# An expert weight stream cut into transfers of 1 MB, each with its own landing semaphore

## The reference, cut to what matters

```python
def expert_rows(args):
    xblk, e = args
    gt = jnp.minimum(xblk @ w_gate[e] + b_gate[e], SWIGLU_LIMIT)
    up = jnp.clip(xblk @ w_up[e] + b_up[e], -SWIGLU_LIMIT, SWIGLU_LIMIT)
    hdn = (up + 1.0) * gt * jax.nn.sigmoid(gt * SWIGLU_ALPHA)
    return hdn @ w_down[e] + b_down[e]
```

## Time and profile before

| what | value |
|---|---|
| median of 3 runs (lowest, highest) | 1259.48 us (1254.93, 1263.06) |
| profiled execution, its own time | 1256.86 us |
| its span, first to last instruction | 1255.0 us |
| mean granted TensorE clock | 0.971 |
| TensorE busy with matmuls | 1169.7 us, 93% |
| VectorE, ScalarE busy | 487.4 us, 197.0 us |
| read from HBM | 443.57 MB |
| chain of waits: PE, DMA, DVE | 63%, 21%, 13% |

### The profile page before, as it was taken

How to read it: one execution, slowest core, us unless ns; L and a number is a source line. 1 busy time by engine, 2 the same in 40 slices (tenths; PEclk the granted TensorE clock), 3 DMA queues, 4 the chain that set the end, 5 groups by cost and what they waited for, 6 DMA issues and landing times.

```text
span 1255.0 us, 20776 instructions
## 1 busy us (share of the span) xinstructions
PE 1169.7 (93%) x8462; PEld 568.1 (45%) x8462; DVE 487.4 (39%) x1090; ACT 197.0 (16%) x432; POOL 5.4 (0%) x33
## 2 busy tenths in 40 slices
PE   8999988999999989888899999999999899999896
PEld 6888767875334333333333433333433334343333
DVE  2999997105332322232222332221333222233233
ACT  2144513012111101011100111100111100111012
POOL 0000000000000000000000000000000000000000
PEclk9999998999999988998999999899999999999989
DMA  9542338924999999999999999999999999999994
GB/s 393 233 171 78 132 130 295 357 109 155 392 403 426 426 426 427 427 426 427 426 427 427 399 428 426 426 426 410 414 426 426 425 428 371 423 426 428 425 427 182
DMA packets 37074, 452.62 MB, mean 361 GB/s; under 512 B 5112, under 2 KB 5656, under 8 KB 10080
## 3 DMA queue, kind: packets, MB, share of 16 engines
q1 hardware_dynamic: 35344, 449.02, 86.0%
q10 hardware_dynamic: 1616, 1.82, 0.4%
HBM read 443.57 MB, written 7.25 MB: 359 GB/s over the span
## 4 chain that ended last, share of the span: by engine, by line
PE 63%; DMA 21%; DVE 13%; issue 2%; DVEq 1%; ACT 0%; POOL 0%; SPq 0%; POOLq 0%; ACTq 0%
PE ps L1556 26%; DMA ring<-in_w_experts 20%; PE ps L1599 9%; DVE acts L777 5%; PE ps L1523 3%; PE ps L1318 3%; PE ps L1425 3%; PE ps L1292 2%; PE ps L1482 2%; PE ps L1608 2%; PE ps L1538 2%; PE ps L1566 2%; PE ps L1416 1%; DVE acts L1137 1%; DVE acts L872 1%
## 5 line engine op out<-in xcount | busy, mean ns | idle before, releaser
L1556 PE MATMUL ps<-ring,extra 128*64 128x512 f32 x1824 | 415.6, 607 | 10.3 <-DMA ring<-in_w_experts 8.0
L1556 PEld LDWEIGHTS ps<-ring,extra 128*64 128x64 f32 x1824 | 127.0, 139 | 276.6 <-issue 260.8
L1599 PE MATMUL ps<-ring,extra 128*32 128x256 f32 x3072 | 191.9, 397 | 21.5 <-DMA ring<-in_w_experts 21.4
L1137 DVE TENSOR_TENSOR acts<-ps,acts 128x528 f32<-128x528 f32 x128 | 85.2, 704 | 261.3 <-PE ps L1566 157.6
L1599 PEld LDWEIGHTS ps<-ring,extra 128*32 128x32 f32 x3072 | 94.3, 113 | 114.8 <-issue 36.0
L777 DVE SCALAR_TENSOR_TENSOR acts<-ring,small,acts 128x256 f32<-128x256 f32 x224 | 91.2, 474 | 1.1 <-ACT acts L489 1.1
L1318 PE MATMUL ps<-acts,ring 128*128 128x280 f32 (+1 forms) x320 | 75.3, 394 | 0.3 <-ACT ring L562 0.3
L1318 PEld LDWEIGHTS ps<-acts,ring 128*128 128x128 f32 x320 | 60.5, 190 | 14.2 <-issue 1.0
L1142 DVE TENSOR_SCALAR extra<-ps 128x512 f32<-128x512 f32 x32 | 22.1, 692 | 114.9 <-PE ps L1556 114.9
L1318 PE MATMUL ps<-acts,extra 128*128 128x280 f32 x256 | 61.3, 400 | 1.9 <-DVE acts L759 1.9
L1151 DVE TENSOR_SCALAR extra<-ps 128x512 f32<-128x512 f32 x32 | 22.1, 689 | 95.5 <-PE ps L1556 78.9
(11 more groups left out here) (307 smaller groups left out, 892.0 us busy)
## 6 DMA issues: line engine op xcount, KB each, us to landing
ring<-in_w_experts SPq DMA_DIRECT2D x192, 2048.0 KB, 28.1
ring<-in_w_in_t SPq DMA_DIRECT2D x5, 2048.0 KB, 21.0
extra<-in_w_in_t SPq DMA_DIRECT2D x4, 2048.0 KB, 11.1
extra<-in_w_out_t SPq DMA_DIRECT2D x4, 1024.0 KB, 5.9
ring<-in_w_out_t SPq DMA_DIRECT2D x4, 1024.0 KB, 6.4
ring<-in_state_t SPq DMA_DIRECT2D x8, 512.0 KB, 7.7
ring<-dtx_rows SPq DMA_DIRECT2D x8, 512.0 KB, 6.4
out_ssm_s_t<-ring SPq DMA_DIRECT2D x8, 512.0 KB, 7.0
```

Source lines behind the costliest of these rows:

```text
L1137: TT(both, ps[:, BACK_BANK[m]:BACK_BANK[m] + 2, 0:TN], both, ALU.add).then_inc(ev["acc_done"], 1)
L1556: hs.append(MM(dst, src[:, o:o + HALF], weight(w, p, k, 512 * h_, 512), start=(fresh and kk == 0), stop=(kk == KT - 1), skip_group_check=T ...
L1599: hs.append(MM(dst, src[:, o:o + QUAR], weight(w, p, k, 256 * q, 256), start=(fresh and kk == 0), stop=(kk == KT - 1), skip_group_check=True))
```

## The change

- A transfer is one piece of 1 MB (8 KB per partition, every other 8 KB of the HBM block of a pair) and no longer a pair of 2 MB. There are 384 of them for 192.
- The landing semaphores belong to the 16 places of the ring (`piece_slot`), one each, and TensorE waits for the one of the piece that it multiplies with.
- `stream` waits for one piece to be used and requests its place. `gate_piece` replaces `gate_half` and `gate_used`: TensorE counts it up after each gate piece, the fourth time at the first up matmul (with one pass) or after the last gate piece (with two). `piece_used` keeps its eight counts per expert.
- `prefetch` requests the two pieces of a pair one behind the other.
- The loop of the stream writes out four experts for two, so that the place in the ring is a constant. Experts 2 and 3 stand ahead of it.
- Two semaphores on which nothing waits (`e_ready`, `sy_ready`) are gone.

```diff
-        landed = [[sem(f"pair_landed{par}_{i}") for i in range(NP // 2)] for par in range(2)]
+        landed = [sem(f"piece_landed{k}") for k in range(NQ * 4)]
...
+        def piece_slot(i, p):
+            return (i * 3 + p // 4) % NQ * 4 + p % 4
+        def piece_row(i, p):
+            k = piece_slot(i, p)
+            return ring[:, k * PIECE:(k + 1) * PIECE]
...
-        def expert_pair(e, q):
-            return expert_w[bass.ds(e, 1), q].rearrange("o p n -> p (o n)")
+        def expert_piece(e, p):
+            return expert_w[bass.ds(e, 1), p // 2, :, p % 2 * PIECE:(p % 2 + 1) * PIECE].rearrange("o p n -> p (o n)")
...
             def prefetch(q, i=0):
-                sp.dma_start(pair_row(i, q), expert_pair(i, q)).then_inc(landed[i][q], 16)
+                for p in (2 * q, 2 * q + 1):
+                    sp.dma_start(piece_row(i, p), expert_piece(i, p)).then_inc(landed[piece_slot(i, p)], 16)
...
-            def stream(i, e, par, first=0):
-                for q in range(first, NP // 2):
-                    if q < 2:
-                        sp.wait_ge(ev["piece_used"], i * 8 - 16 + 6 + 2 * q)
-                    elif q < 4:
-                        sp.wait_ge(ev[("gate_half", "gate_used")[q - 2]], i)
+            def stream(i, at, e, first=0):
+                for p in range(first, NP):
+                    if p < 4:
+                        sp.wait_ge(ev["piece_used"], i * 8 - 11 + p)
+                    elif p < 8:
+                        sp.wait_ge(ev["gate_piece"], i * 4 - 7 + p)
                     else:
-                        sp.wait_ge(ev["piece_used"], i * 8 - 8 + 2 * (q - 3))
-                    sp.dma_start(pair_row(i, q), expert_pair(e, q)).then_inc(landed[par][q], 16)
-            stream(1, 1, 1, 2)
+                        sp.wait_ge(ev["piece_used"], i * 8 - 15 + p)
+                    sp.dma_start(piece_row(at, p), expert_piece(e, p)).then_inc(landed[piece_slot(at, p)], 16)
+            stream(1, 1, 1, 4)
             sp.wait_ge(ev["order_ready"], 1)
-            with sp.Fori(0, NE // 2 - 1) as ii:
-                for par in range(2):
-                    e = sp.value_load(order[0:1, bass.ds(ii * 2 + 3 + par, 1)], min_val=0, max_val=NE - 1)
-                    stream(ii * 2 + 2 + par, e, par)
+            for i in (2, 3):
+                stream(i, i, sp.value_load(order[0:1, i + 1:i + 2], min_val=0, max_val=NE - 1))
+            with sp.Fori(0, NE // 4 - 1) as t:
+                for h in range(4):
+                    e = sp.value_load(order[0:1, bass.ds(t * 4 + 5 + h, 1)], min_val=0, max_val=NE - 1)
+                    stream(t * 4 + 4 + h, h, e)
...
             def piece_products(p, b, src, bank, fresh, w):
-                pe.wait_ge(w[1][p // 2], w[2])
+                pe.wait_ge(*w[1][p])
...
             def gate_of(n, w, then):
                 for p in range(4):
                     hs = piece_products(p, 0, xT, 0, False, w)
-                    if n == 1 and p == 1:
-                        hs[-1].then_inc(ev["gate_half"], 1)
+                    if n == 1 and p < 3:
+                        hs[-1].then_inc(ev["gate_piece"], 1)
```

More of the change, by code:

```diff
@@ L217, in build @@
                  "dtc_out dt_mm dt_v dt_exp dt_ready ctap_ready conv_done xtap_ready xtail_out xconv_done xs_pre xa_ready z_out "
-                 "acum_mm meta_v meta_exp decb_ready xtok_mm xdt_ready cb_mm d_ready e_ready ce_ready m_ready xdec_ready "
+                 "acum_mm meta_v meta_exp decb_ready xtok_mm xdt_ready cb_mm d_ready ce_ready m_ready xdec_ready "
                  "y_mm st_mm y_ready hT_ready hT_out kept_out mean_mm cent_ready csq_ready var_mm lr_ready norm_ready conf_ready "
-                 "xs_tr dtx_ready dtx_out sh_new sh_y sy_ready yg_ready ysq_ready yvar_mm yr_ready yn_ready "
+                 "xs_tr dtx_ready dtx_out sh_new sh_y yg_ready ysq_ready yvar_mm yr_ready yn_ready "
                  "wo_y_landed wo_conf_landed wo_used wo_mm acc_ready h_tr hsq_ready hstd_ready xn_ready lg_mm nm_ready topexp "
@@ L223, in build @@
                  "rows_zeroed rows_loaded xg_done sg_tr pick_done gp_ready sc_done gate_done g_ready hdn_ready "
-                 "y_back p_ready acc_done s_ready rank_ready sg_ready sort_mm order_ready o_list sig_ready gate_used gate_half up_first piece_used o_tab f_ready f_out fsq_ready fss_mm frstd_ready iota_ready").split()
+                 "y_back p_ready acc_done s_ready rank_ready sg_ready sort_mm order_ready o_list sig_ready gate_piece up_first piece_used o_tab f_ready f_out fsq_ready fss_mm frstd_ready iota_ready").split()
         ev = {n: sem(n) for n in names}
-        landed = [[sem(f"pair_landed{par}_{i}") for i in range(NP // 2)] for par in range(2)]
+        landed = [sem(f"piece_landed{k}") for k in range(NQ * 4)]
         win_landed = [sem(f"win_landed{i}") for i in range(5)]
@@ L404, in _ @@
                         sp.wait_ge(ev["piece_used"], j * 8 + NE * 8)
-                        for q in range(NP // 2):
-                            sp.dma_start(pair_row(0, q), expert_pair(e, q)).then_inc(landed[0][q], 16)
+                        for p in range(NP):
+                            sp.dma_start(piece_row(0, p), expert_piece(e, p)).then_inc(landed[p], 16)
             for q in range(4):
@@ L990, in _ @@
             last = yT[:, :, SEQ:TN]
-            TT(last, ps[:, 7, 0:KT * NB].rearrange("p (m b) -> p m b", m=KT), sdt, ALU.add).then_inc(ev["sy_ready"], 1)
+            TT(last, ps[:, 7, 0:KT * NB].rearrange("p (m b) -> p m b", m=KT), sdt, ALU.add)
             v.drain()
@@ L1140, in gate_in @@
                 for b in range(2):
-                    v.wait_ge(ev[("gate_done", "gate_used")[b]], n + 1)
+                    if b == 0:
+                        v.wait_ge(ev["gate_done"], n + 1)
+                    else:
+                        v.wait_ge(ev["gate_piece"], n * 4 + 4)
                     TS(ge[:, 512 * b:512 * (b + 1)], ps[:, b, :], LIMIT, None, ALU.min).then_inc(ev["g_ready"], 1)
@@ L1539, in bias, with weights_of @@
                        start=True, stop=False, skip_group_check=True)
-            def weights_of(i, par, n16):
-                return [matrix_at(i, m) for m in range(3)], landed[par], n16
+            def weights_of(i):
+                return ([matrix_at(i, m) for m in range(3)],
+                        [(landed[piece_slot(i, p)], 16 * ((i * 3 + p // 4) // NQ + 1)) for p in range(NP)])
             def weight(w, p, k, c, n):
-                return span(w[0][p // 4] + (p % 4) * PIECE + k * D + c, n)
+                at = w[0][p // 4] + (p % 4) * PIECE + k * D + c
+                return ring[:, at:at + n]
             def piece_products(p, b, src, bank, fresh, w):
-                pe.wait_ge(w[1][p // 2], w[2])
+                pe.wait_ge(*w[1][p])
                 hs = []
@@ L1690, in up_of @@
                         if p == 4:
-                            hs[0].then_inc(ev["gate_used"], 1)
+                            hs[0].then_inc(ev["gate_piece"], 1)
                         hs[-1].then_inc(ev["up_first" if p == 7 else "piece_used"], 1)
@@ L1697, in up_of @@
                         hs = piece_products(p, 1, xT, 0, False, w)
-                        if p % 2:
-                            hs[-1].then_inc(ev[("gate_half", "gate_used")[p // 2]], 1)
+                        hs[-1].then_inc(ev["gate_piece"], 1)
                     for p in range(4, 8):
@@ L1731, in gate_s @@
                         then()
-                    if p == 1:
-                        hs[-1].then_inc(ev["gate_half"], 1)
+                    if p < 3:
+                        hs[-1].then_inc(ev["gate_piece"], 1)
                     if p == 3:
@@ L1833, in first_back @@
                 find_order()
[L1835 to L1838, removed]
+            big_expert(0, weights_of(0), first, first_back, second, True)
+            big_expert(1, weights_of(1), second, lambda: big_back(1, first), None)
+            small_expert(2, weights_of(2), lambda: big_back(2, second), None)
+            small_expert(3, weights_of(3), lambda: small_back(3), count_of(5))
             now = count_of(5)
@@ L1841, in _ @@
                 coming = count_of(i + 3)
-                big_expert(i, weights_of(i, 0, i // 2 * 16 + 16), now, lambda: small_back(i), None)
-                small_expert(i + 1, weights_of(i + 1, 1, i // 2 * 16 + 16), lambda: big_back(i + 1, now), coming)
+                big_expert(i, weights_of(i), now, lambda: small_back(i), None)
+                small_expert(i + 1, weights_of(i + 1), lambda: big_back(i + 1, now), coming)
                 now = coming
@@ L1877, in _ @@
                         bias(2, 96)
-                        w = [0, MAT, 2 * MAT], landed[0], j * 16 + 8 * NE + 16
+                        w = [0, MAT, 2 * MAT], [(landed[p], j * 16 + 16 * (3 * NE // NQ + 1)) for p in range(NP)]
                         gate_of(2, w, lambda: None)
```

## The result

The changed kernel takes 1266.55 us (median of 8 runs, 1263.45 to 1272.27) against 1257.6 us for the kernel before (8 runs, 1251.78 to 1263.06). The ratio is 1.008, with a 95% interval of 1.0058 to 1.0103. It is 8.95 us slower; forecast was 5.1 us faster. The difference is small, but the interval leaves no change out: the forecast had the sign wrong.

What follows compares the result with a forecast made beforehand. The weight stream at 427 GB/s, its losses in four stretches and a fixed tail bound the kernel. Gains at restarts and landings less 0.8% packet cost gave -5.1 us: 1254.5 us against the 1259.5 median, range 1246 to 1270.

Steps and rivals of the forecast that it cites:

- The packets' cost: Weight stream: 8 KB packets in place of 16 KB slow it by 0.8%, taken between 0.4% and 1.4%.
- The sum of the prediction: Stream and TensorE shifts followed to the kernel's end: -5.1 us; -0.2 us with packets at 1.4%.
- The later restarts: Three slow stretches behind the wide experts: 2.06, 2.48 and 4.45 us lost, regained except where TensorE bounds it.
- the bounded part: Fourth stretch, near 1070 us: TensorE limits the regain, so the stream's shift is -5.48 us instead of -5.81.
- The first restart: Stretch near 364 us: one megabyte less waits behind the late request, 2.46 us gained.
- The last landing: End of the weight stream: one small piece left to multiply instead of two, 1.0 us gained.
- Edits costed at nothing: 192 further requests at 0.34 us each on SyncE, prefetch requests, longer loop and waits: hidden, no cost.
- the rival for the slower side: Weight stream: 8 KB packets cost 5.1% on every 2 MB, +32 us in all, 1289 us; chance 0.12.
- The 5.1% of the earlier trace: Start of a transfer into an idle queue: 324.5 ns per 8 KB packet, 5.1% over; outer bound of packet cost.

Runs made afterwards that it cites:

- The split kernel: Kernel before, with only the third of an expert's six pairs requested and landed as two 1 MB transfers; 1256.24 us against 1256.65, ratio 1.0.
- the first experiment: Kernel before with weights laid piece by piece in HBM, so its 2 MB transfers move 8 KB packets; 1267.04 us, ratio 1.0079.
- the even and odd split: Kernel before with each pair moved by two 1 MB transfers of 16 KB packets, for even and odd partitions; 1257.41 us, ratio 0.9996.

## Why the prediction was wrong

What follows counts landings: the time at which the n-th megabyte of expert weights had landed, from the landing semaphores in the traces. Both traces have the clock at 1.00 in 296 to 304 us (first trace of before, second of the changed kernel). The plateau's pace is taken between megabytes 48 and 128; "over the plateau's pace" is the time that a stretch took beyond its megabytes at that pace.

```
                                              before   changed   difference
16th megabyte landed (us)                      296.9     298.1      +1.2
16th to 48th, over the plateau's pace (us)      22.49     19.67     -2.8
plateau, us per megabyte                         2.4785    2.5222   +0.0437
   16th to 48th: x 32                                               +1.4
   48th to 384th: x 336                                            +14.7
48th to 384th, over the plateau's pace           6.71      2.11     -4.6
   of it 160th to 192nd                          0.89      0.24
         232nd to 264th                          0.98      0.19
         288th to 328th                          2.27     -0.09
last landing                                  1238.19   1248.06     +9.9
from there to the end of the span               16.8      15.2      -1.6
span                                          1255.0    1263.3      +8.3
```

**The packets' cost** is the step that failed first: the mechanism was the right one, the term was mis-sized, and its size decides the sign. I took 0.8% between 0.4 and 1.4; the stream is 0.0437/2.4785 = 1.8% slower per megabyte here and 1.6% in the first trace of the changed kernel (2.5184). That is some 15 us over the 336 megabytes where 7.0 us stood. The rows had the answer. A quiet window and the real stream differ by 617.7 - 611.8 = 5.9 ns per packet. I read this as a property of the stream and set the quiet 8 KB packet between the two. But the load adds it to each packet of either size: 2 x (310.2 + 5.9) = 632.2 ns, and 631.0 were measured. The packets' own durations in the traces say the same: from a quiet window to the stream the mean of a 16 KB packet goes from 611.0 to 616.3 ns, that of an 8 KB packet from 309.5 (before) to 314.3 (changed). Like had to be compared with like. The sum of the prediction at 1.6% gives about +1.5 us, and the sign is open.

**The later restarts** are the second. I took 2.06, 2.48 and 4.45 us as lost there, from the rates in windows of 20 us, and let all but the bounded part come back. By the landings only 0.89, 0.98 and 2.27 us lay above the pace of the plateau (the plateau's pace already has the packets of the "instruction" queue in it). The second trace of before gives 0.50, 0.72 and 2.04. The split kernel shows the same disagreement, 3.7 us by the window and 0.3 by the landings. The rate and the share are means over 16 engines, and a transfer has landed when its last engine is done. Engines that are ahead may run dry and cost nothing. The packets in the trace bear no engine, but the 16 counts of a transfer's landing do come apart: in the kernel before the first and the last lie 3.5 us apart in the median from 400 to 600 us and up to 7.5 us behind the first later wide expert. A stretch of 2 us without work on some engines fits into that; that it costs nothing is not shown. What was there did come back, 3.8 of 4.14 us. But part came by the slower stream: with 8 KB packets and the requests of before (the first experiment) 0.72, 0.49 and 0.37 us are left, and with 1 MB transfers requested late 0.38, 0.50 and 0.03. A stream that is late finds the ring less full: that is how I read it.

**The first restart** came out as forecast: 2.8 us for 2.46, and 26.0 - 23.7 = 2.4 us in the other two traces, both with the clock at 0.79. These are single traces, and the same restart moves by 3 to 4 us with the clock. **The last landing** was right too, a piece where a pair stood: its matmuls took 1.07 us for 1.93. Two more things differ behind it: the closing sums (3.83 against 5.51 us for the same 16 matmuls, at a granted clock of 1.00 against 0.72), and some 1 us more from there to the end.

**Edits costed at nothing.** The 0.34 us for a request did not hold: it became 1.8 in the median. That a held SyncE would cost nothing is borne out for the plateau: the kernel with 8 KB packets in 2 MB transfers and the changed one, held for 0.74 and 1.81 us in the median, have the same 420 GB/s. The doubled number of transfers is free to within some 3 us, by the even and odd split. Not foreseen was the longer stall marked "issue", some 4 us of TensorE in all. What of it reaches the end isn't shown. At a clock of 1.00 the piecewise requests and landings gain 1267.0 - 1263.3 = 3.7 us over the same packets in 2 MB transfers, in one pair of traces; the medians, 1266.55 and 1267.04 us, do not show it. So the change is two in one: packets +12 us by trace (1267.0 - 1255.0), +10 us by medians, and places released and landed by the megabyte, somewhere between 0 and -4.

**The rivals.** The packets were the rival for the slower side, and the mechanism was the right one, at 1.6 to 1.8% and not at 5.1%. The 5.1% of the earlier trace rows were no price of a packet in a stream: the median packet of 8 KB took 309 ns there as in the earlier trace rows, and some slower ones raised the mean. The rule of the Trainium skill, page "DMA: Bandwidth & Descriptors", section "Anatomy of one DMA", that a DMA carries some 2 us of fixed cost, was measured there for DMAs that GpSimd issues. It does not show in this stream, where SyncE issues them and many are under way: 192 more transfers with packets of 16 KB cost nothing that shows (0.9996, 0.9975 to 1.0018). The same page of the Trainium skill, section "Why small descriptors are slow", names a fixed overhead of about 3 cycles per packet and 32 bytes of descriptors per DMA operation, and works it out for 256 bytes; here each further packet of 8 to 32 KB costs some 14 ns, a price that the section does not give.

## What to carry to other kernels

In a stream that keeps the DMA engines busy, the contiguous run per partition moves the rate (420, 426 and 430 GB/s for 8, 16 and 32 KB here), and the number of transfers does not: before a transfer is cut, cut it so that the runs stay long, and count a fixed price per packet, measured under the load it will run in. Finer requests can help only where the queue runs empty; read that from the landing times over a long stretch, not from a rate in a short window. And part of what a finer grain can win back is gone already when its price slows the stream, since a slower stream finds fewer full rings.

## What the runs showed of the hardware that was not expected

- The time went per packet, not per transfer or completion: 1221.0 ns for 32 KB, 617.7 for 16 KB, 315.5 for 8 KB in the loaded stream (430, 426 and 420 GB/s).
- Loads into 64 neighbouring partitions, lower and upper half in turn, ran at half the rate with all engines busy (216 GB/s, 1220.6 ns for 16 KB); into every other partition they ran at full rate (426 GB/s, 617.8 ns).
- Requests held SyncE in the kernels with 8 KB packets, in 2 MB transfers (median 738 ns, longest 7387) as in 1 MB (median 1814), and with 384 transfers of 64 packets of 16 KB they did not (median 497). So it seems to go by the packets under way; at which number is open.
- TensorE's granted clock fell near 300 us in some executions of a program and not in others (0.79 or 1.00 over 296 to 304 us); the spans differ by some 3 us.
